# Where the stage buffers start in SBUF: one padding line taken out of a three-layer fp32 kernel

## The chip, the cores and the metric

The program runs on one core of one Trainium2 chip. The metric is the device time of one execution in microseconds. Three runs of the kernel before took 2893.61, 2891.4 and 2893.53 us, with a median of 2893.53 us. The execution that the profiler recorded is the one of 2893.61 us.

## The reference, cut to what matters

The input is x, 1024 tokens by 1024 channels in fp32. Three layers run one after the other.

```
# layer 1: RG-LRU beside latent attention (8 heads), gated
proj = x @ ab_w_in                       -> x_rnn, gate, c_q, c_kv, k_rope
y_rnn = scan of x_rnn (conv, two gates, h = a*h + u)
y_mla = softmax(q k^T) v, causal, q and k from rmsnorm(c_q), rmsnorm(c_kv)
x = layernorm(ALPHA*x + (concat(y_rnn, y_mla) * silu(gate)) @ ab_w_out)
# layer 2: state-space layer, 4 groups of 8 heads, chunks of 128 tokens
proj = x @ ssd_w_in                      -> z, xs, B, C, dt
y = chunked scan(xs, dt, B, C) + d*xs;   y = groupnorm(y * silu(z))
x = layernorm(ALPHA*x + y @ ssd_w_out)
# layer 3: short convolution beside stick-breaking attention, then a wide MLP
h = x + concat(conv_out, attn) @ w_out,  from rmsnorm(x) @ w_in
h = h + relu(rmsnorm(h) @ w_up)^2 @ w_down          # 1024 -> 4096 -> 1024
h = h + sigmoid(rmsnorm(h) @ w_ple_gate) * (p @ w_ple_proj)
out = rmsnorm(h)
```

## The kernel before

Activations are kept transposed: channels on the 128 partitions, tokens along the free axis, so that 1024 x 1024 is eight tiles of 128 x 1024. Every fp32 matrix that takes part in a large product is split into a high part of type fp32r and the fp32r remainder, and a product is three passes: high weights by high activations, high weights by low activations, low weights by high activations. `product` (its matmul is line 566) does this for one slab of weights: 8 tiles by 3 passes by 2 halves of 512 tokens, 48 matmuls.

All weights are laid out as `NSLAB` slabs of 128 x 1024 floats, in the order in which they are used. SyncE loads slab n into one of two slots of `w_stage`, GpSimd splits it into `w_hi` and `w_lo` (lines 486 and 488), TensorE uses it, and VectorE or ScalarE empties the pair of PSUM banks. Each engine has its program written out in order by hand, with semaphores between them, and no scheduler chooses anything. In the MLP of layer 3 TensorE takes four slabs of `w_up` (activations `raw_hi` and `raw_lo`, in the code XH2 and XL2) and four of `w_down` (activations `ffn_u_hi` and `ffn_u_lo`, UH and UL) in turn, eight times.

SBUF is laid out by hand too. `place` puts a tile at a byte offset of each partition and rounds the end up to a multiple of 128 bytes. `sb` places at the running offset `base[0]`. The tiles that stay for the whole program come first: `w_stage`, `w_hi`, `w_lo`, `H`, `XH`, `XL` (the residual stream and its two parts), the column vectors `VC`, the constant matrices `CN`, `RW`, three small bf16 matrices, `SM`, and `after_r` (AFTER_R, line 189), a 128 x 128 fp32r matrix. Everything that belongs to one stage is then placed from `base[0]` on, each stage over the last one: `rnn_*`, `mla_*`, `trig`, `latent_roots`, `cq`, `x_again`, `norm_*`, all of `ssd_*`, `ple_p*`, `ple_proj_tiles`, all of `sb_*`, `head_sq`, `conv_gated`, `rest_r`, `ffn_t`, `square_sum`, `root`, `raw_hi` and `raw_lo`. Some stage tiles lie instead inside the areas of H, XH and XL, as `cq_hi`, `ckv_hi`, `ffn_u_hi`, `ffn_u_lo`, `ple_proj_a`, `out_tiles`, `conv_out` and `attn_out`.

In this document the phase of a tile is its start offset in a partition modulo 256 bytes. From the sizes in the code, with the first tile at byte 16,512, the phases before are these. `w_stage`, `w_hi`, `w_lo`, `H`, `XH`, `XL`, `VC` and `SM` have phase 128. `CN`, `RW` and `after_r` have phase 0; `from_r` is placed over `after_r` and has it too. `after_r` starts at 146,688 and ends at 147,200. Line 190 then moves `base[0]` on to 147,328, so that the stage tiles start there. Every stage tile but `mla_sums` has phase 128. Inside a tile the slices that the engines read start mostly at multiples of 512 bytes, so a slice has its tile's phase; `ssd_dt` is read in slices of 8 columns, 32 bytes apart, and `ssd_a_hi` and `ssd_a_lo` likewise.

Of the kernel before, what the change touches and what calls it, by code (L numbers as in the profile page):

```python
# [13 lines left out]
P = 128  # L14
# [130 lines left out]
def program(nc, x_t, pos, w, vec, rows, consts, p_t, out):  # L145
    ctx = ExitStack()
    with ctx:
        base = [(nc.sbuf_base + 127) // 128 * 128]
# [6 lines left out]
        def sb(name, shape, dt=F32):  # L155
            t, base[0] = place(base[0], name, shape, dt)
            return t
# [29 lines left out]
        SM = sb("SM", [P, 10, 8])  # L187
        after_at = base[0]
        AFTER_R = sb("after_r", [P, P], F32R)
        base[0] = after_at + P * 4 + (P - (after_at + P * 4)) % 256  # L190
        EPS5, EPS6 = SM[:, 0, 6:7], SM[:, 0, 7:8]
        XH_f, XL_f = XH[:, :, :].bitcast(F32), XL[:, :, :].bitcast(F32)

# [2323 lines left out]
def build(nc, arrays):  # L2517
    args = [nc.dram_tensor(k, a.shape, mybir.dt.from_np(a.dtype), kind="ExternalInput").ap() for k, a in arrays.items()]
    out = nc.dram_tensor("out_t", (KT, P, TOK), F32, kind="ExternalOutput").ap()
    program(nc, *args, out)  # L2520
# [12 lines left out]
```

## Time and profile before

| what | value |
|---|---|
| median of three runs | 2893.53 us |
| the profiled execution | 2893.61 us |
| its span in the trace | 2891.8 us |
| outside the span | 1.8 us |
| PE (matmul) busy | 2713.7 us, 94% of the span |
| PEld (weight load) busy | 2166.7 us, 75% |
| DVE (VectorE) busy | 1568.7 us, 54% |
| ACT (ScalarE) busy | 924.9 us, 32% |
| POOL (GpSimd) busy | 739.0 us, 26% |
| DMA, mean rate | 47 GB/s |
| mean granted TensorE clock | 0.981 of full |

Times are microseconds of one profiled execution. PE is TensorE's matmuls and PEld its weight loads, which run beside them. A busy share is an average over stages; the chain that ended last is what set the time. Matmuls overlap in the pipeline, so that the mean duration of one (some 390 ns for 512 columns) is longer than the distance from one to the next.

### The profile page before, as it was taken

What the parts mean: (1) busy time and instruction counts of PE and PEld (TensorE: products, weight loads), DVE (VectorE), ACT (ScalarE), POOL (GpSimd) and SP (SyncE); (2) the same over time, 40 slices, a digit from 0 to 9 for tenths busy, and PEclk for the clock granted to TensorE, in tenths of its full rate; (3) what the DMA queues carried; (4) which work ended last, traced back from release to release, by engine and by line L of the source; (5) the groups of instructions that cost most, each with busy time, mean ns of one, the idle gap of its engine ahead of it and who ended that gap; (6) DMA issues with size and microseconds to landing.
All of it is one profiled execution on the core that took longest, in us unless ns stands there. A gap on an engine that the chain in (4) does not pass through costs nothing.

```text
span 2891.8 us, 31232 instructions
## 1 busy us (share of the span) xinstructions
PE 2713.7 (94%) x12558; PEld 2166.7 (75%) x12558; DVE 1568.7 (54%) x1666; ACT 924.9 (32%) x1144; POOL 739.0 (26%) x414
## 2 busy tenths in 40 slices
PE   8999989789999999998989899988999999999997
PEld 6877778577787787886656667766888888888885
DVE  5636663568758758758755565665422222222266
ACT  2527770412201211212256566565220011100032
POOL 2432322121231221321121111111423333233231
PEclk9999999999999999999999999999999999999998
DMA  3110003011110110111130100002111111111211
GB/s 127 48 50 24 23 21 97 15 44 30 31 51 23 37 52 15 44 44 37 51 120 27 30 22 30 29 22 80 44 51 46 49 51 44 51 51 44 96 60 71
DMA packets 38145, 136.27 MB, mean 47 GB/s; under 512 B 4144, under 2 KB 4272, under 8 KB 38000
## 3 DMA queue, kind: packets, MB, share of 16 engines
q1 hardware_dynamic: 28224, 102.77, 11.9%
q10 hardware_dynamic: 9776, 31.45, 2.9%
q8 instruction: 105, 1.72, 0.2%
q14 instruction: 40, 0.33, 0.0%
HBM read 121.63 MB, written 12.58 MB: 46 GB/s over the span
## 4 chain that ended last, share of the span: by engine, by line
PE 80%; DVE 11%; ACT 6%; issue 3%; POOL 0%; DMA 0%; ACTq 0%; DVEq 0%; POOLq 0%
PE PS L566 65%; PE PS L873 2%; PE PS L789 1%; PE PS L875 1%; PE PS L681 1%; DVE sb_softplus L2244 1%; DVE ssd_decay L2034 1%; PE PS L880 1%; PE PS L710 1%; DVE mla_neg_max L1848 1%; PE PS L1063 1%; PE PS L1024 1%; PE PS L861 1%; PE PS L695 1%; PE PS L1041 1%
## 5 line engine op out<-in xcount | busy, mean ns | idle before, releaser
L486 POOL CAST w_hi<-w_stage 128x1024 fp32r<-128x1024 f32 x196 | 210.4, 1074 | 1948.5 <-PE PS L566 1857.3
L566 PE MATMUL PS<-XH,w_hi 128*128 128x512 f32 x1536 | 493.1, 402 | 34.0 <-DVE ssd_conv L2085 9.2
L488 POOL TENSOR_TENSOR w_lo<-w_stage,w_hi 128x1024 fp32r<-128x1024 f32 x196 | 486.2, 2481 | 15.7
L566 PE MATMUL PS<-XL,w_hi 128*128 128x512 f32 x1536 | 479.1, 393 | 0.0
L566 PE MATMUL PS<-XH,w_lo 128*128 128x512 f32 x1536 | 478.4, 393 | 0.0
L566 PEld LDWEIGHTS PS<-XH,w_hi 128*128 128x128 f32 x1536 | 284.1, 191 | 100.7 <-issue 40.8
L566 PEld LDWEIGHTS PS<-XL,w_hi 128*128 128x128 f32 x1536 | 292.0, 190 | 63.3
L566 PEld LDWEIGHTS PS<-XH,w_lo 128*128 128x128 f32 x1536 | 291.2, 190 | 62.5
L1674 ACT ACTIVATE ffn_t<-ffn_t 128x1024 f32<-128x1024 f32 x32 | 34.0, 1063 | 530.6 <-DVE ffn_t L2294 530.6
L566 PE MATMUL PS<-raw_hi,w_hi 128*128 128x512 f32 x624 | 192.9, 390 | 0.0
L566 PE MATMUL PS<-raw_lo,w_hi 128*128 128x512 f32 x624 | 192.1, 389 | 0.0
L566 PE MATMUL PS<-raw_hi,w_lo 128*128 128x512 f32 x624 | 192.1, 389 | 0.0
L2294 DVE SCALAR_TENSOR_TENSOR ffn_t<-PS,root 128x1024 f32<-128x1024 f32 x32 | 39.2, 1225 | 218.9 <-PE PS L566 210.9
L566 PE MATMUL PS<-ffn_u_lo,w_hi 128*128 128x512 f32 x512 | 157.6, 389 | 0.0
L566 PE MATMUL PS<-ffn_u_hi,w_lo 128*128 128x512 f32 x512 | 157.6, 389 | 0.0
L566 PE MATMUL PS<-ffn_u_hi,w_hi 128*128 128x512 f32 x512 | 157.6, 389 | 0.0
L566 PEld LDWEIGHTS PS<-raw_hi,w_hi 128*128 128x128 f32 x624 | 117.1, 188 | 25.1 <-issue 1.0
L566 PEld LDWEIGHTS PS<-raw_lo,w_hi 128*128 128x128 f32 x624 | 117.1, 188 | 24.4
L566 PEld LDWEIGHTS PS<-raw_hi,w_lo 128*128 128x128 f32 x624 | 117.1, 188 | 24.3
L566 PEld LDWEIGHTS PS<-ffn_u_hi,w_lo 128*128 128x128 f32 x512 | 96.1, 188 | 20.0
L566 PEld LDWEIGHTS PS<-ffn_u_lo,w_hi 128*128 128x128 f32 x512 | 96.1, 188 | 20.0
L566 PEld LDWEIGHTS PS<-ffn_u_hi,w_hi 128*128 128x128 f32 x512 | 96.1, 188 | 19.9
(378 smaller groups left out, 4417.0 us busy)
## 6 DMA issues: line engine op xcount, KB each, us to landing
w_stage<-w SPq DMA_DIRECT2D x196, 512.0 KB, 3.6
H<-x_t ACTq DMA_DIRECT2D x4, 1024.0 KB, 11.0
x_again<-x_t ACTq DMA_DIRECT2D x8, 512.0 KB, 3.7
pj_kept<-ple_proj_tiles ACTq DMA_DIRECT2D x8, 512.0 KB, 3.3
h_kept<-H ACTq DMA_DIRECT2D x8, 512.0 KB, 2.7
H<-h_kept ACTq DMA_DIRECT2D x4, 1024.0 KB, 5.3
out_t<-out_tiles ACTq DMA_DIRECT2D x16, 256.0 KB, 3.5
ple_proj_a<-pj_kept ACTq DMA_DIRECT2D x1, 2048.0 KB, 8.6
```

What stands on the lines that cost most here:

```text
L486: nc.gpsimd.tensor_copy(w_hi[:, slot, :, :], w_stage[:, slot, :, :]).then_inc(s_w_hi, 1)
L488: nc.gpsimd.tensor_tensor(w_lo[:, slot, :, :], w_stage[:, slot, :, :], w_hi[:, slot, :, :].bitcast(F32), ALU.subtract).then_inc(s_w_ready, 1)
L566: mm = nc.tensor.matmul(outs[:, half, :], wt[:, slot, k, :], a[:, k - first, half * HB:(half + 1) * HB], start=(k == whole[0] and wt is w_ ...
L681: nc.tensor.matmul(PS[:, b + lo // HB, 0:hi - lo], qq[:, u % 2, j * P:(j + 1) * P], kk[:, u % 2, lo:hi], start=(qq is QH and kk is KH), st ...
L695: mm = nc.tensor.transpose(PS[:, 4 + n % 2, at_:at_ + P], PB[:, MLA_ROWS.index(j) % 4, kt * P:(kt + 1) * P], CN[:, C_ID, :])
L710: mm = nc.tensor.matmul(PS[:, b, q0 + late:q0 + 2 * P], VM[:, u % 2, 2 * p + e, :], src[:, n % 4, 2 * P * e:2 * P * (e + 1) - late], start ...
L789: mm = nc.tensor.matmul(PS[:, 6 + half, :], CN[:, C_ONES, :], SQN[:, k % 2, half * HB:(half + 1) * HB], start=(k == 0), stop=(k == KT - 1))
L861: mm = nc.tensor.matmul(PS[:, 6 + b, :], AFTER_R[:, :], a[:, 4 * b:4 * b + 4, :].rearrange("p h l -> p (h l)"), start=(a is AVH), stop=(a ...
L873: nc.tensor.matmul(PS[:, 2, 64 * h:64 * h + 64], E[:, c % 2, h, :], XF[:, c % 2, 64 * h:64 * h + 64], start=True, stop=True)
L875: mm = nc.tensor.matmul(PS[:, 3, :], CT[:, tok], ST[:, :], start=True, stop=True)
L1674: nc.scalar.activation(FT[:, c % 2, :], FT[:, c % 2, :], ACT.Square).then_inc(s_fq, 1)
L2294: v.scalar_tensor_tensor(out=FT[:, c % 2, :], in0=flat(n % 2), scalar=0.0, in1=RSQ[:, :], op0=ALU.max, op1=ALU.mult).then_inc(s_evac[n % 2 ...
```

## The change

One line is taken out. The running offset is no longer moved on after `after_r`.

```diff
--- before
+++ after
@@ -187,7 +187,6 @@
         SM = sb("SM", [P, 10, 8])
         after_at = base[0]
         AFTER_R = sb("after_r", [P, P], F32R)
-        base[0] = after_at + P * 4 + (P - (after_at + P * 4)) % 256
         EPS5, EPS6 = SM[:, 0, 6:7], SM[:, 0, 7:8]
         XH_f, XL_f = XH[:, :, :].bitcast(F32), XL[:, :, :].bitcast(F32)
```

Without the line `base[0]` stays at the end of `after_r`, 147,200, a multiple of 256. So every stage tile that is placed from `base[0]` starts 128 bytes earlier, and its phase becomes 0 (that of `mla_sums`, 16 floats, becomes 128). The tiles that stay for the whole program, and the stage tiles inside H, XH and XL, stay where they are, at phase 128 or, for `CN`, `RW`, `after_r` and `from_r`, at 0. The distance between two stage tiles doesn't change. The sequence of instructions on each of the five engines, with their shapes and their waits, is the same row for row before and after; only addresses differ, and line numbers behind line 190 are one lower.

## Rows read from the trace of the kernel before

**Rows 1.** The page, part 4, the chain that ended last by engine and line

```profile
PE 80%; DVE 11%; ACT 6%; issue 3%; POOL 0%; DMA 0%; ACTq 0%; DVEq 0%; POOLq 0%
...
PE PS L566 65%; PE PS L873 2%; PE PS L789 1%; PE PS L875 1%; PE PS L681 1%; DVE sb_softplus L2244 1%; DVE ssd_decay L2034 1%; PE PS L880 1%; PE PS L710 1%; DVE mla_neg_max L1848 1%; PE PS L1063 1%; PE PS L1024 1%; PE PS L861 1%; PE PS L695 1%; PE PS L1041 1%
```

**Rows 2.** Busy time, granted clock and DMA share by stretch of the span

```profile
core 0: us, PE busy (x) PEld busy (x) DVE busy (x) ACT busy (x) POOL busy (x), PEclk, DMA share, GB/s
...
640.00:1440.00 800.00, 766.02 (x3620) 611.74 (x3619) 590.91 (x647) 160.03 (x176) 181.78 (x103) 0.99 0.13 38
...
2090.00:2790.00 700.00, 700.00 (x3086) 578.97 (x3085) 182.84 (x143) 88.40 (x83) 220.26 (x128) 1.00 0.18 55
```

**Rows 3.** Two pieces of the chain in order of time: start, us, what

```profile
768.08 97.95 PE PS L566 x432
...
2094.14 696.33 PE PS L566 x3072
```

**Rows 4.** TensorE groups by form, products on weight slabs; busy us, mean ns

```profile
L566 PE MATMUL PS<-XH,w_lo 128*128 128x512 f32 x1536 | 478.4, 393 | 0.0
...
L566 PE MATMUL PS<-raw_hi,w_hi 128*128 128x512 f32 x624 | 192.9, 390 | 0.0
...
L566 PE MATMUL PS<-ffn_u_hi,w_lo 128*128 128x512 f32 x512 | 157.6, 389 | 0.0
...
L566 PE MATMUL PS<-ssd_y_hi,w_lo 128*128 128x512 f32 x256 | 79.7, 393 | 0.0
```

**Rows 5.** TensorE groups by form, weights at phase 0 and at phase 128

```profile
L861 PE MATMUL PS<-ssd_a_upto_lo,after_r 128*128 128x512 f32 x64 | 25.2, 394 | 0.0
...
L1041 PE MATMUL PS<-sb_softplus_hi,from_r 128*128 128x512 f32 x48 | 16.0, 416 | 4.5 <-DVE sb_softplus_lo L2246 4.5
...
L1041 PE MATMUL PS<-sb_softplus_lo,from_r 128*128 128x512 f32 x48 | 15.5, 404 | 0.0
...
L1052 PE MATMUL PS<-sb_softplus_hi,rest_r 128*128 128x512 f32 x32 | 10.7, 416 | 9.3 <-DVE sb_z L2240 9.3
...
L1052 PE MATMUL PS<-sb_softplus_lo,rest_r 128*128 128x512 f32 x32 | 10.0, 392 | 0.0
```

**Rows 6.** TensorE groups by form, two products of 128 columns

```profile
L849 PE MATMUL PS<-ssd_c,ssd_b 128*128 128x128 f32 x64 | 12.6, 277 | 0.0
...
L850 PE MATMUL PS<-CN,ssd_b 128*128 128x128 f32 x32 | 8.7, 272 | 0.0
```

**Rows 7.** VectorE, lines 2009 and 1992: count, min/median/max ns, first and last start

```profile
L2009 DVE TENSOR_TENSOR ssd_xdt<-PS,ssd_dt x32: 680/681/682, 661.8 to 1346.8; 128x512 f32<-128x512 f32 x32
...
L1992 DVE TENSOR_TENSOR ssd_a_upto_hi<-CN,ssd_a_hi x32: 1224/1224/1227, 657.1 to 1339.1; 128x1024 fp32r<-128x1024 f32 x32
L1992 DVE TENSOR_TENSOR ssd_a_upto_lo<-CN,ssd_a_lo x32: 1218/1218/1221, 658.2 to 1340.3; 128x1024 fp32r<-128x1024 f32 x32
```

**Rows 8.** VectorE group by form, one addition with both operands in SBUF

```profile
L2105 DVE TENSOR_TENSOR H<-H,ssd_y_rows 128x1024 f32<-128x1024 f32 x12 | 14.7, 1225 | 0.4
```

**Rows 9.** ScalarE groups by form, plain copies into XH

```profile
L1191 ACT ACTIVATE XH<-H 128x1024 fp32r<-128x1024 f32 x8 | 8.0, 1050 | 5.5 <-DMA H<-x_t 5.5
...
L1384 ACT ACTIVATE XH<-norm_t 128x1024 fp32r<-128x1024 f32 x8 | 8.5, 1063 | 9.9 <-DVE norm_t L1951 8.7 <-ACT ple_proj_tiles L1500 1.2
```

**Rows 10.** DMA issues: count, KB each, us to landing

```profile
x_again<-x_t ACTq DMA_DIRECT2D x8, 512.0 KB, 3.7
...
pj_kept<-ple_proj_tiles ACTq DMA_DIRECT2D x8, 512.0 KB, 3.3
...
latent_roots<-pos ACTq DMA_DIRECT2D x1, 256.0 KB, 3.4
```

**Rows 11.** Who waited for whom: us in total, times, longest

```profile
DVE trig L1798 <- DMA latent_roots<-pos: 12.4, 1, 12.4
...
DVE H L1929 <- PE PS L566: 49.6, 8, 9.7
```

## The prediction

> **What bounds the kernel now.** I read the shares of the chain that ended last first, since only what stands on it can move the time: TensorE holds 80% of it and the slab products of line 566 alone 65%; VectorE holds 11%, ScalarE 6%, DMA 0% [rows 1]. Then the stretches: in the MLP, 2090 to 2790 us, TensorE is busy for 700.00 of 700 us at a granted clock of 1.00, and in the state-space layer, 640 to 1440 us, for 766 of 800 us [rows 2]. Then the chain in order of time, where the MLP is one unbroken piece of 3072 matmuls in 696.33 us, 226.7 ns from one to the next, and a projection of the state-space layer is 432 in 97.95 us, again 226.7 ns [rows 3]. The reader should see how stiff this is: the two stretches stand beside quite different work of VectorE, GpSimd and the DMA queues, and the distance is the same to a tenth of a nanosecond. So the time is the number of matmuls by their distance, and a change that adds or removes no instruction must act on the speed of single instructions.
>
> **What the change does.** It removes no instruction, wait or transfer and moves none past another. It starts each stage tile 128 bytes earlier, from phase 128 to phase 0. Three things are new: the absolute phase of the stage tiles; the relation of stage tiles to the tiles that stay (before, nearly every pair of SBUF operands had equal phase 128; now `raw_hi` at 0 meets `w_hi` at 128); and the alignment of four kinds of transfer. The semaphores are the same, so no wait is added and nothing new is queued behind one. I cost it engine by engine.
>
> **TensorE, the term that decides.** Moving operands whose relation to their weights changes: `raw_hi` and `raw_lo`, three groups of 624, that is 1872 matmuls; `ssd_y_hi` and `ssd_y_lo`, three of 256, 768 [rows 4]; by the code another 192 (48 of the recurrent gates at line 603, 48 of the last gate slab at line 1166, 96 of `ple_p` at line 955). Together 2832 matmuls of 512 columns. `XH`, `XL` and `ffn_u` keep their place. What would one cost? The trace of before has a case of mixed phases, because `after_r` and `from_r` are weights at phase 0 with moving operands at 128, while `rest_r` is the same kind of matrix at 128 with the same moving operand. Three pairs, mixed against equal: `ssd_a_upto_lo` with `after_r` 394 ns against 393 for `ssd_y_hi` with `w_lo`; `sb_softplus_hi` 416 with `from_r` against 416 with `rest_r`; `sb_softplus_lo` 404 against 392 [rows 4, 5]. So mixed costs +1, 0 and +12 ns. The +12 stands in a stretch where TensorE starts and stops and the durations include the pipeline; I take 0, the value of the two pairs that are tighter, and keep +12 as the upper end: 2832 by 12 ns is +34 us.
>
> The other side is the absolute phase of the moving operand. With `ssd_b` as the stationary one, a product of 128 columns with `ssd_c` (phase 128) moving takes 277 ns, and one with `CN` (phase 0) moving 272 ns [rows 6]. The second is a transpose and not the same form, so the 5 ns are a bound and not a price: 2832 by -5 ns is -14 us. Between -14 and +34 I take 0.
>
> **VectorE.** Line 2009 reads `ssd_dt` in slices 32 bytes apart, so that its 32 executions start at eight different phases in turn: 680 to 682 ns. Line 1992 reads `CN` at phase 0 together with such slices of `ssd_a_hi` and `ssd_a_lo`: 1224 to 1227 and 1218 to 1221 [rows 7]. A start at another phase thus costs VectorE at most 2 of 681 ns, 0.3%, and by its 11% of the span, 318 us, that is 1 us either way. The additions that go from equal to mixed are of the kind of line 2105, H (128) with `ssd_y_rows`, at 1225 ns with equal phases [rows 8]; line 1992 with mixed ones and the same length takes 1224. I take 0.
>
> **ScalarE.** No ScalarE row isolates the phase. Copies of one length into XH spread from 1050 to 1063 ns at equal phase [rows 9], 1.2%; taken as a bound in both directions on ScalarE's 6% of the span, 174 us, it gives 2 us either way. I take 0, since an effect of the memory's address that neither of the two other engines shows has no row to lean on.
>
> **GpSimd and the weights.** `w_stage`, `w_hi` and `w_lo` are not moved, so the weight pipeline, its loads included, is as before: 0. GpSimd has 220 of 700 us in the MLP [rows 2] and would have to become more than three times as slow to be late.
>
> **DMA.** Transfers whose SBUF side moves: `x_again` 8 by 3.7 us, `ple_proj_tiles` out 8 by 3.3, `ple_p` 5.1, `latent_roots` 3.4, together 64.5 us [rows 10]. None is waited for on the chain: the one that reads `x_again` waits for TensorE, 49.6 us, and the only wait for one of the four is line 1798 for the positions, 12.4 us of VectorE [rows 11]. DMA has 0% of the chain [rows 1]. If the cover were gone the whole 12.4 us would be the stake, and a transfer of 3.4 us can give back only a part of 3.4. I take 0, with -1 to +1 us.
> The Trainium skill (DMA: Bandwidth & Descriptors, "How a descriptor splits into AXI transactions") says that a transfer that doesn't start at a multiple of 256 bytes fetches the block below its start too. By that page a row of 4096 bytes takes 132 beats from phase 128 and 128 from phase 0; my estimate from it is 3% of the 64.5 us, 2 us, in favour of the change, and all of it beside other work. No run so far shows it.
>
> **Sum.** 0 (TensorE) + 0 (VectorE) + 0 (ScalarE) + 0 (GpSimd) + 0 (DMA): 2891.8 us of span and 1.8 us around it, 2893.6 us; the profiled execution is the one that ran longest of the three, 0.1 us over their median, 2893.5 us, which I take.
>
> **Rivals.**
> - *Slower: mixed phases cost TensorE.* Place: the slab products with `raw_hi`, `raw_lo` and `ssd_y` as moving operands, 2640 of the 2832, on the chain without slack [rows 3]. For it: the pair 404 against 392, and that nearly all operands of before share one phase, so the trace can hide it. Against it: the other two pairs, +1 and 0, and VectorE's mixed line 1992. Price: the mean of the three pairs, 4.3 ns, by 2832 gives +12 us, 2906 us; at the full 12 ns 2927 us. It decides from 2 ns a matmul, which makes 5.7 us or 0.2%.
> - *Faster: streams that start at a multiple of 256 are shorter.* A row of 512 floats, 2048 bytes, covers nine blocks of 256 bytes from phase 128 and eight from phase 0. For it: 272 against 277 ns [rows 6]. Against it: VectorE's insensitivity in steps of 32 bytes [rows 7], and that the distance of 226.7 ns looks like a fixed number of columns and not like memory. Price: -14 us, 2879 us.
> - *The line changes nothing that the chip can tell apart.* Then it is my forecast, 2893.5 us, within some 3 us, a little over what the three runs spread (2.2 us).
>
> **How the numbers follow.** What a measurement of this kernel can tell from no change is about 0.2%, 5.8 us. Forecast 68%, the slower rival 18%, the faster 14%; the small bounds of VectorE, ScalarE and DMA, together 4 us, stay inside 0.2%, so the three chances are also those of same, slower and faster. The range of the likeliest case alone is 2890 to 2897. For 8 in 10 it must take in about half of each rival's weight: 2885 to 2905.
>
> **What would show it.** Right: the piece of 3072 matmuls again lasts 696.3 us within 0.3; the groups of `raw_hi` stay at 390 ns and those of `ffn_u`, which serve as a control because they were not moved, at 389; line 2009 at 681, line 2105 at 1225. The slower rival: `raw_hi` and `ssd_y` groups rise and `ffn_u` doesn't, and the weight loads beside them rise too. The faster: they fall, the `ffn_u` ones don't. What I would have missed entirely is a VectorE or ScalarE operation between a stage tile at 0 and a staying tile at 128 that takes visibly longer than before in the start-and-stop stretches, 200 to 640 and 1440 to 1960 us, or a changed meeting of VectorE with GpSimd.

## The result, and the profile after

The changed kernel takes 2908.4 us in the median of five runs (2906.37 to 2908.87), against 2892.48 us for the kernel before in the runs beside it. The ratio is 1.0053, with a 95% interval of 1.0042 to 1.0065, or 12 to 19 us more. That is slower, where no change was forecast, and it lies just above the stated range of 2885 to 2905 us. The span of the profiled execution went from 2891.8 to 2907.3 us.

A projection of the state-space layer and the MLP, each as one piece of the chain in order of time (start, us, what), which answer to [rows 3]:

```profile
768.68 99.08 PE PS L565 x432
...
2098.10 706.32 PE PS L565 x3072
```

The same 3072 matmuls last 706.32 us and not 696.33: 10.0 us more. The 432 take 99.08 us and not 97.95; 192 of them have `ssd_y` as moving operand, so that is 5.9 ns for each of these. Still there is no gap: in the MLP row of the stretch table TensorE is busy throughout, at a granted clock of 1.00 before and after, so the engine got slower without waiting for anyone and without a lower clock. Over the whole span too TensorE was busy at the lower clock for about the same time, 76.1 us before and 76.7 after.

```profile
640.00:1440.00 800.00, 767.40 (x3613) 610.96 (x3613) 587.94 (x645) 156.75 (x173) 182.37 (x104) 0.99 0.12 38
2090.00:2790.00 700.00, 700.00 (x3043) 571.06 (x3042) 175.14 (x139) 83.46 (x79) 216.81 (x126) 1.00 0.18 55
```

Which matmuls? The TensorE groups by form (busy us, mean ns of one), beside [rows 4]:

```profile
L565 PE MATMUL PS<-XH,w_lo 128*128 128x512 f32 x1536 | 478.2, 393 | 0.0
...
L565 PE MATMUL PS<-raw_hi,w_hi 128*128 128x512 f32 x624 | 196.9, 396 | 0.0
L565 PE MATMUL PS<-raw_hi,w_lo 128*128 128x512 f32 x624 | 196.2, 395 | 0.0
L565 PE MATMUL PS<-raw_lo,w_hi 128*128 128x512 f32 x624 | 196.1, 395 | 0.0
...
L565 PE MATMUL PS<-ffn_u_hi,w_lo 128*128 128x512 f32 x512 | 157.5, 389 | 0.0
...
L565 PE MATMUL PS<-ssd_y_hi,w_lo 128*128 128x512 f32 x256 | 81.5, 400 | 0.0
```

The groups whose moving operand was shifted against its weights rose by 6 to 7 ns, `raw_hi` with `w_hi` from 390 to 396 and `ssd_y_hi` with `w_lo` from 393 to 400. Those that stayed in place, `XH` and `ffn_u`, read 393 and 389 as before. `raw` and `ffn_u` alternate in the same 700 us, so `ffn_u` is as good a control as one program can hold. It is not a few slow matmuls but all of them, as the shortest, median and longest duration of one group show, before and after:

```profile
L566 PE MATMUL PS<-raw_lo,w_hi x624: 389/389/389, 2081.8 to 2856.6; 128*128 128x512 f32 x156
```

```profile
L565 PE MATMUL PS<-raw_lo,w_hi x624: 390/393/404, 2085.5 to 2872.2; 128*128 128x512 f32 x156
```

In all, the three raw groups grew by 12.1 us of busy time and the three `ssd_y` groups by 5.1 us; the span grew by 15.5.

The operations of VectorE that I had named didn't move. Their rows beside [rows 7] and [rows 8] are these (count, min/median/max ns in the first; busy us and mean ns in the second).

```profile
L2008 DVE TENSOR_TENSOR ssd_xdt<-PS,ssd_dt x32: 680/681/682, 662.4 to 1351.3; 128x512 f32<-128x512 f32 x32
```

```profile
L2104 DVE TENSOR_TENSOR H<-H,ssd_y_rows 128x1024 f32<-128x1024 f32 x12 | 14.7, 1226 | 0.4
```

### The profile page after: what moved, and what is told of

It reads as the page before. It is cut to its first block, busy times and chain, and to the rows that moved or that the text cites. A ratio compares the mean times of both kernels' runs of the same rounds, so it can differ in the third digit from the quotient of the medians.

```text
span 2907.3 us, 31232 instructions
## 1 busy us (share of the span) xinstructions
PE 2730.6 (94%) x12558; PEld 2167.3 (75%) x12558; DVE 1571.3 (54%) x1666; ACT 923.5 (32%) x1144; POOL 739.1 (25%) x414
## 4 chain that ended last, share of the span: by engine, by line
PE 81%; DVE 10%; ACT 5%; issue 3%; POOL 0%; DMA 0%; ACTq 0%; DVEq 0%; POOLq 0%
PE PS L565 66%; PE PS L872 2%; PE PS L788 1%; PE PS L874 1%; PE PS L680 1%; DVE sb_softplus L2243 1%; DVE ssd_decay L2033 1%; PE PS L709 1%; PE PS L879 1%; PE PS L1062 1%; DVE mla_neg_max L1847 1%; PE PS L1023 1%; PE PS L860 1%; PE PS L694 1%; PE PS L667 1%
```

## The experiments

Two theories could make these rows. By A the relation counts: a matmul is slow when its moving operand and the weights differ in phase. By B the absolute phase counts: a moving operand at phase 0 is slow. In the changed kernel both say the same.

**The staying tiles at 0, the stage tiles at 128** (the mirror image of the change).

```diff
--- changed kernel
-        base = [(nc.sbuf_base + 127) // 128 * 128]
+        base = [(nc.sbuf_base + 127) // 128 * 128 + 128]
```

> The changed kernel with all tiles placed 128 bytes later: the staying tiles (w_hi, w_lo, H, XH, XL and with them ffn_u) get phase 0, the stage tiles phase 128. Theory A (relation): a matmul is slow where its moving operand and the weights that are loaded beside it differ by 128 in phase. Then XH and ffn_u with w (0 with 0) stay at 226.7 ns from one matmul to the next, mean 389; raw and ssd_y (128 with 0) stay slow at some 233 ns, mean 395; time as after the change, 2908 us, within 3. Theory B (absolute): a moving operand at phase 0 is slow by itself. Then raw and ssd_y are fast again, and XH, XL and ffn_u, some 6100 matmuls, are slow by 6.2 ns: about +38 us on before, 2931 us.

Measured: ratio to before 1.0063 (1.0046 to 1.0079), 2909.16 us.

```profile
L565 PE MATMUL PS<-raw_hi,w_lo 128*128 128x512 f32 x624 | 196.1, 395 | 0.0
...
L565 PE MATMUL PS<-ffn_u_hi,w_hi 128*128 128x512 f32 x512 | 157.7, 389 | 0.0
```

`ffn_u` now starts at phase 0 with weights at 0 and stays at 389 ns; `raw` has phase 128 again, as in the fast kernel before, and is slow, at 395. Theory B falls.

**The weight tiles alone at 0.**

```diff
--- changed kernel
+        RW = sb("RW", [P, 96])
         w_stage = sb("w_stage", [P, 2, 8, P])
 ...
         w_lo = sb("w_lo", [P, 2, 8, P], F32R)
+        SM = sb("SM", [P, 10, 8])
         h_at = base[0]
 ...
-        RW = sb("RW", [P, 96])
 ...
-        SM = sb("SM", [P, 10, 8])
```

> The changed kernel with two small tiles (RW and SM, each an odd multiple of 128 bytes) put around the weight tiles, so that w_stage, w_hi and w_lo get phase 0 and nothing else changes its phase against the changed kernel but RW and SM. Theory A (relation): raw and ssd_y (0 with 0) are back at 226.7 ns; XH, XL and ffn_u (128 with 0), some 6100 matmuls, go to 233 ns: about +38 us on before, 2931 us. Theory B (absolute phase of the moving operand): nothing changes against the changed kernel, 2908 us, raw slow and ffn_u fast.

Measured: 1.0108 (1.0091 to 1.0125), 2921.11 us, 31.6 us over before (median 2889.55 us on that chip).

```profile
L565 PE MATMUL PS<-XH,w_lo 128*128 128x512 f32 x1536 | 486.0, 397 | 0.0
...
L565 PE MATMUL PS<-raw_lo,w_hi 128*128 128x512 f32 x624 | 192.2, 389 | 0.0
L565 PE MATMUL PS<-raw_hi,w_lo 128*128 128x512 f32 x624 | 192.1, 389 | 0.0
L565 PE MATMUL PS<-ffn_u_lo,w_hi 128*128 128x512 f32 x512 | 161.2, 395 | 0.0
```

The roles are exchanged: `raw` is fast, `ffn_u` slow, by moving neither, only the weights. That is theory A again. The loss was forecast 6 us too high: `XH` and `XL` lost 4.5 ns a matmul (20.7 us of busy time over 4608), not the 6.9 of `ffn_u` (10.6 us over 1536). Why they lost less, no run shows. By the code the edit changes the phase of the three small bf16 matrices too, beside that of `RW` and `SM`, which the expectation leaves out; the slab products read none of them.

**`raw_hi` and `raw_lo` alone put back.**

```diff
--- changed kernel
-            ("raw_hi", [P, KT, TOK], F32R), ...
+            ("gap", [P, 32], F32), ("raw_hi", [P, KT, TOK], F32R), ...
```

> The changed kernel with raw_hi and raw_lo alone put back to phase 128 by a gap of 128 bytes ahead of them. Theories A and B both: raw at 389 ns again, ssd_y still near 395 to 400. 1920 matmuls by 6.3 ns come back, 12 us of the 16: 2896 us, within 2. If the loss came from something else than these streams (timing between engines, another stage tile), less than half of it comes back: 2902 us or more.

Measured: 1.0028 (1.0018 to 1.0039), 2897.91 us.

```profile
2101.12 696.37 PE PS L565 x3072
```

```profile
L565 PE MATMUL PS<-ssd_y_hi,w_lo 128*128 128x512 f32 x256 | 82.0, 402 | 0.0
```

The MLP is back at 696.4 us, and the rest of the loss stayed with `ssd_y`. What is left, 5 to 11 us, is more than the 4 that I expected. The `ssd_y` groups took 6.6 us more here than in the kernel before, against 5.1 more in the changed kernel, but not because a product cost more: from one start to the next in unbroken stretches (distances under 300 ns) both kernels have a mean of 232.6 ns, and the kernel before 226.7. The rest is the clock. Of these 768 matmuls 13 lasted over 600 ns at a granted clock of 0.50 in the kernel before, 16 in the changed kernel and 24 here, most of them 628 ns in place of some 390, and each took some 0.2 us longer to the next.

**Pairs of phases by themselves.** This kernel leaves the whole computation out. Once VectorE has filled the tiles with zeros TensorE works alone, and for a kind of pair it repeats

```
for n in range(96):
    matmul(PS[:, n % 2, :], wt[:, n // 2 % 4, :], mov[:, n % 2 * 512:(n % 2 + 1) * 512])
```

> A kernel of its own that leaves out the whole computation: TensorE streams 512 columns again and again, each matmul with its own weight load, 96 of a kind, over pairs of start phases. mov_a is at 128, mov_b at 0, mov_c to mov_h at 160, 192, 224, 32, 64, 96 and mov_i at 144; wt_p is at 128, wt_z at 0. Theory A: a with p and b with z take 226.7 ns from one to the next, b with p and a with z 233. Theory B: b is slow with both, a with neither. In the two alternating series each matmul has first weights of its own phase while the next ones loaded beside it have the other phase, then the reverse. If the cost is a clash in time of stream and next load, the first is slow (233) and the second fast; if it is a property of the pair that is multiplied, the first is fast and the second slow. Distances between: if only bit 7 of the address counts, the other distances give parts of the cost, growing towards 128 bytes; if lines of 32 bytes count, no distance but 0 is fast. For bf16 and for plain fp32 no theory gives a number; with bf16 half the bytes are read and I expect no cost.

The groups of one execution (busy us, mean ns). With no gap in a series, the distance from one matmul to the next is the busy time less one mean duration, over the count less one.

```profile
L190 PE MATMUL PS<-mov_fua,wt_fup 128*128 128x512 f32 x96 | 41.4, 592 | 0.0
L190 PE MATMUL PS<-mov_fub,wt_fup 128*128 128x512 f32 x96 | 41.4, 592 | 0.0
...
L190 PE MATMUL PS<-mov_f,wt_p 128*128 128x512 f32 x96 | 22.6, 396 | 0.0
...
L190 PE MATMUL PS<-mov_c,wt_p 128*128 128x512 f32 x96 | 22.6, 395 | 0.0
...
L190 PE MATMUL PS<-mov_d,wt_p 128*128 128x512 f32 x96 | 22.1, 391 | 0.0
L190 PE MATMUL PS<-mov_bfb,wt_bfp 128*128 128x512 bf16 x94 | 20.8, 379 | 0.1
L190 PE MATMUL PS<-mov_bfa,wt_bfp 128*128 128x512 bf16 x94 | 20.6, 379 | 0.1
```

From the starts in the trace: 128 apart takes 233.3 ns whichever of the two is at 0, equal phases 226.8; 32 bytes above the weights (c) 233.4, 64 above (d) 228.9, 96 above (e) 233.5, 32 below (h) 233.2, 64 below (g) 233.3, 96 below (f) 234.1. Plain fp32 takes 429.2 ns at equal phase and at 128 apart, and bf16 379 ns as the duration in both with a commonest distance of 216. So the cost belongs to fp32r here. The two alternating series were meant to tell the own weights from the next ones; they gave 228.4 and 230.0 ns, between fast and slow both times, and decide nothing.

**All stage tiles 64 bytes later, and 64 bytes earlier, than in the kernel before.** The pair kernel says that the sign counts.

```diff
--- kernel before
         base[0] = after_at + P * 4 + (P - (after_at + P * 4)) % 256
+        base[0] += 64        # in the other run: -= 64
```

> The kernel before with all stage tiles 64 bytes later, at phase 192, while w_hi and w_lo stay at 128. Theory A1 (any unequal phase costs, by the amount that the pair kernel showed for its distance): with 64 bytes above the weights a matmul took 228.9 ns from one to the next there, 2.1 more than at equal phase. So 1920 raw and 768 ssd_y matmuls cost 6 us, and the run is 0.2% above before. Theory A2 (only bit 7 of the address tells two classes apart): phase 192 has the same bit 7 as 128, no cost, same time as before.

> The kernel before with all stage tiles 64 bytes earlier, at phase 64. Theory A1: 64 bytes below the weights the pair kernel took 233.3 ns, 6.6 more than at equal phase, as much as at 128: some +17 us on before, raw at a mean of 395 ns. Theory A2: bit 7 differs, the same +16 us. Both with ffn_u at 389. If the distance alone counted and not its sign, this run would equal the one with 64 bytes more.

Measured: 1.0030 (1.0018 to 1.0041) for 64 later and 1.0072 (1.0055 to 1.0089) for 64 earlier. The MLP piece of the run with 64 later, then of the one with 64 earlier:

```profile
2095.80 700.20 PE PS L567 x3072
```

```profile
2098.58 706.70 PE PS L567 x3072
```

Over the 1536 raw matmuls in the piece that is 2.5 ns and 6.8 ns each, where the pair kernel had 2.1 and 6.6. With 64 bytes more the three raw groups don't agree with each other, though moving tiles and weights have the same two phases in all three: 390 ns (`raw_hi` with `w_lo`), 392 (`raw_hi` with `w_hi`) and 393 (`raw_lo` with `w_hi`). So the difference of the phases doesn't fix the cost to the nanosecond; what else enters is open. The theory that bit 7 of the address alone counts (A2) falls: phase 192 shares it with 128 and still costs. In the whole program both came out somewhat above the forecast, 8.7 and 20.8 us by the ratios against 6 and 17; both forecasts lie in the lower parts of the intervals (5 to 12, 16 to 26).

**All phases equal** (but for `SM` and the three small bf16 matrices, which go from 128 to 0).

```diff
--- kernel before
+        base[0] += 128
         CN = sb("CN", [P, NCONST, P])
 ...
-        base[0] = after_at + P * 4 + (P - (after_at + P * 4)) % 256
```

> The kernel before with its 128 bytes of padding put ahead of CN and not behind after_r, so that after_r and from_r, which are weights for moving operands at phase 128, have phase 128 too, and CN as well. Theory A: the products with after_r and from_r, some 290 of 512 columns, lose the 3 to 6 ns that unequal phases cost, 1 to 2 us in all, 0.05%, too little for the total time to tell; in the trace from_r groups fall from 416 and 404 ns to some 409 and 399. The products of plain fp32 with CN don't move. Theory B would see no change in them, since their moving operands were at 128 all along.

Measured: 0.9998 (0.9988 to 1.0008), 2891.15 us: no difference, as expected, and so no kernel better than the one before.

```profile
L1041 PE MATMUL PS<-sb_softplus_hi,from_r 128*128 128x512 f32 x48 | 15.6, 408 | 4.5 <-DVE sb_softplus_lo L2246 4.5
L1041 PE MATMUL PS<-sb_softplus_lo,from_r 128*128 128x512 f32 x48 | 15.2, 400 | 0.0
L1052 PE MATMUL PS<-sb_softplus_hi,rest_r 128*128 128x512 f32 x32 | 11.2, 432 | 9.5 <-DVE sb_z L2240 9.5
L1052 PE MATMUL PS<-sb_softplus_lo,rest_r 128*128 128x512 f32 x32 | 10.4, 406 | 0.0
```

`from_r` fell to 408 and 400 ns as forecast, but `after_r` didn't move (437 and 394 ns before and here), which stays open. `rest_r`, whose own relation to its moving operand is the same as before, rose from 416 and 392 to 432 and 406. One burst of four matmuls is the whole of that rise. Here it is in the kernel before and then in this run (start, us, what), with the row of the stretch table for each:

```profile
1944.29 0.73 PE L1052 MATMUL PS<-sb_softplus_hi,rest_r 128*128 128x512 f32 x2 [2.49 <-DVE sb_z L2240]
1944.85 0.62 PE L1052 MATMUL PS<-sb_softplus_lo,rest_r 128*128 128x512 f32 x2
...
1944.28:1945.30 1.02, 1.01 (x4) 0.67 (x4) 1.02 (x1) 1.02 (x1) 0.00 (x0) 1.00 0.83 245
```

```profile
1943.04 1.22 PE L1052 MATMUL PS<-sb_softplus_hi,rest_r 128*128 128x512 f32 x2 [2.48 <-DVE sb_z L2240]
1944.06 1.06 PE L1052 MATMUL PS<-sb_softplus_lo,rest_r 128*128 128x512 f32 x2
...
1943.03:1945.69 2.66, 2.65 (x8) 1.73 (x10) 1.54 (x2) 2.58 (x3) 0.00 (x0) 0.50 0.63 185
```

The four took 497, 393, 397 and 389 ns at a granted clock of 1.00, and 796, 632, 632 and 632 ns at 0.50. Spread over 32 matmuls a group that is 17 and 15 ns. TensorE had been idle for 2.5 us before the burst in both; the clock had fallen at 1941.9 us here, ahead of the burst, and fell at 1945.6 us in the kernel before, behind it. So the mean of a group in such a stretch mixes matmuls at two clocks.

**How long the two streams are.**

> The pair kernel again (the whole computation left out), 192 matmuls of a kind, each kind with its own moving tile. a with p and d with z are equal phases, b with p and c with z 128 apart; then weights p (128) with moving starts 4 bytes (e), 16 bytes (f), 64 bytes (g) above, 64 below (h), 256 (i) and 512 bytes (j) above. Theory A1: i and j as a, 226.7 ns from one to the next, the others between 228 and 234; A2: e, f and g as a. Then weight tiles of 64 columns, equal (k) and 128 apart (l), and of 32 columns, equal (m) and apart (n); and moving lengths of 384 columns, equal (s) and apart (t), and of 256 (u, v). If the cost is a clash of the moving stream with the load of the next weights, a shorter load clashes less: 6.6 ns with 128 columns, about half with 64 and a quarter with 32. If it belongs to the start of the moving stream, it stays 6.6 ns with all loads and lengths. If it grows with the stream's length, 384 columns show 5 ns and 256 columns 3.3.

The groups of one execution; the distances in the text are again from the starts.

```profile
L189 PE MATMUL PS<-mov_e,wt_p 128*128 128x512 f32 x192 | 45.6, 399 | 0.0
...
L189 PE MATMUL PS<-mov_b,wt_p 128*128 128x512 f32 x192 | 45.0, 395 | 0.0
...
L189 PE MATMUL PS<-mov_l,wt_p 128*64 128x512 f32 x192 | 44.5, 394 | 0.0
L189 PE MATMUL PS<-mov_n,wt_p 128*32 128x512 f32 x192 | 44.4, 393 | 0.0
L189 PE MATMUL PS<-mov_k,wt_p 128*64 128x512 f32 x192 | 44.3, 392 | 0.0
...
L189 PE MATMUL PS<-mov_i,wt_p 128*128 128x512 f32 x192 | 43.7, 389 | 0.0
L189 PE MATMUL PS<-mov_d,wt_z 128*128 128x512 f32 x192 | 43.7, 389 | 0.0
L189 PE MATMUL PS<-mov_j,wt_p 128*128 128x512 f32 x192 | 43.7, 389 | 0.0
L189 PE MATMUL PS<-mov_t,wt_p 128*128 128x384 f32 x192 | 34.0, 338 | 0.0
L189 PE MATMUL PS<-mov_s,wt_p 128*128 128x384 f32 x192 | 33.4, 334 | 0.0
L189 PE MATMUL PS<-mov_u,wt_p 128*128 128x256 f32 x192 | 23.2, 283 | 0.0
L189 PE MATMUL PS<-mov_v,wt_p 128*128 128x256 f32 x192 | 22.9, 281 | 0.0
```

Starts 256 and 512 bytes apart (i, j) are as fast as equal ones (d), so the relation is modulo 256. Even 4 bytes (e) cost, 236.7 ns from one to the next and the most of all. With 384 columns the 128 bytes cost 2.7 ns (176.0 against 173.4), with 256 columns nothing (118.7, the unequal pair being the faster, against 120.0). With weight tiles of 64 columns equal and unequal phases take 230.0 and 231.1 ns, with 32 columns 231.6 and 230.7. So a shorter load doesn't bring the unequal pair down to 226.7 in step with its length; it takes the advantage away from the equal pair. None of my three expectations (a part in proportion, a constant 6.6, in proportion to the stream) fits. What is shown: with a full load of 128 columns, starts that agree modulo 256 save 6.6 ns of a stream of 512 columns and 2.7 of one of 384; with a stream of 256, or with a load of 64 or 32 columns, the two kinds of pair lie within 1.3 ns of each other. That the two read streams meet in some structure of SBUF of that period is my reading, and no run here shows that structure.

## Why the prediction was wrong, by its own steps

- *What bounds the kernel* held: the loss lies in the slab products on the chain, nearly one for one (17.2 us of busy time in the raw and `ssd_y` groups, 15.5 of span). That a change of addresses must act on single instructions held too.
- *TensorE, the term that decides*, is the step that failed. I counted 2832 matmuls that go from equal to unequal phases, rightly, and priced them at 0 where they cost 6.5 ns in the MLP (10.0 us over 1536) and 5.9 in the `ssd_y` products of a projection (1.13 us over 192). I didn't count those with `after_r` and `from_r`, 224 of 512 columns, which go the other way; in the changed kernel the groups with `from_r` fell from 416 and 404 ns to 409 and 399, and `ssd_a_upto_lo` with `after_r` from 394 to 391.
- The price came from three mean durations [rows 5] in stretches where TensorE starts and stops. The +12 ns, 404 with `from_r` against 392 with `rest_r`, was mostly the clock: two of the 48 matmuls behind the 404 took 628 ns at a granted clock of 0.50, the other 46 had a mean of 394, and none of the 32 behind the 392 was that slow. What was left, +2 ns, was no price either, and calling the pairs that gave 0 and +1 "tighter" was picking.
- The trace of before did hold the price, in another quantity. From a `from_r` matmul of 512 columns to the next start none of 83 distances (those under 300 ns) is the steady 226 or 227 ns; in the run with all phases equal 64 of 81 are. `rest_r`, at equal phase all along, has 15 of 44 in the kernel before, so something else lengthens distances in these bursts too.
- The +5 ns that I weighed for a faster stream from phase 0 [rows 6] compared a transpose with a product. With `ssd_c` itself at phase 0, in the changed kernel, the product takes 279 ns, no less than the 277 of before. The mirror run shows the same for long streams: `ffn_u` 389 ns at phase 128 and at 0.
- I read the steady 226.7 ns as insensitivity to memory. All those streams shared one phase; a number that doesn't vary in a trace where its cause doesn't vary says nothing on that cause. The prediction named this itself (nearly all operands share one phase, so the trace can hide it) and gave it too little weight.
- The slower rival named the mechanism, the place, the sign and the control (`ffn_u` not rising). Its price, 4.3 ns and 2906 us, was a third too low, and that it came so near was luck, since some three quarters of it came from the two matmuls at the lower clock. 18% was too small a chance, and the range ended 3 us short of the result. One mark of it was wrong: the weight loads beside the slow matmuls didn't rise; with `raw_hi` they read 188 ns before and after.
- VectorE, ScalarE, GpSimd and DMA at 0 held within what the rows can show: 681 and 1226 ns for the two kinds of operation on VectorE, its busy time 1571.3 us after 1568.7 (two operations on four columns of `SM`, a tile that didn't move, took 0.96 and 2.23 us in place of 0.16), ScalarE's 923.5 after 924.9, GpSimd's 739.1 after 739.0, and `x_again` landing in 3.6 us for 3.7. By the Trainium skill (DMA: Bandwidth & Descriptors, "How a descriptor splits into AXI transactions") aligned rows take fewer beats. No run here shows it: the run with all phases equal has `x_again` at phase 128 again, and it landed in 3.6 us there too, so two runs at one phase differ by as much as the 3% would be, 0.1 us.

The Trainium skill (SBUF — State Buffer, "Who interferes with whom") gives TensorE two read ports of SBUF, one for the moving operand and one for weight loads, and calls them independent. These runs don't bear out for fp32r that the two reads leave each other alone: 226.7 ns against 233.3 by nothing but the relation of the two start addresses.

## What to carry to other kernels

When every tile of a trace has the same alignment, the trace can't price alignment; measure the pair by itself, by the distance between starts in an unbroken stream and not by mean durations in bursts, where a few matmuls at the lower clock can move a mean by more than the effect. For fp32r products of 512 columns with a full weight load per matmul, place activations and weights so that their starts agree modulo 256 bytes: it was worth 3% of such a stream and 0.5% of this program (measured with the weights at phases 128 and 0, and for the other distances at 128 alone). Tiles that are moved, a buffer added or a constant made larger can cost this without any other sign than a few nanoseconds a matmul, at full clock and with no gap.

## What the runs showed of the hardware that I had not expected

- fp32r, 512 columns, 128 x 128 load each: 226.7 ns from one matmul to the next at starts equal modulo 256 bytes; with the moving start above the weights' 236.7 at 4 bytes, 231.6 at 16, 233.4 at 32, 228.9 at 64, 233.5 at 96; below them 233.2 at 32, 233.3 at 64, 234.1 at 96; and 233.3 at 128. bf16 and plain fp32 showed no such cost at 128.
- At 128 apart the slow distance is not even: in the MLP of the changed kernel the two halves of a tile are followed by 237 to 238 and by 229 ns in turn.
- A smaller weight load made the equal-phase stream slower, from 226.7 ns with 128 columns to 230.0 with 64 and 231.6 with 32.
- At a granted clock of 0.50 a matmul of that form lasted 628 to 632 ns, 427 from one start to the next, where the same burst at 1.00 had 389 to 397 and some 230.
